# A decoder step on one core: V and K projections in eight slices of two channel tiles instead of four quarters of four

## The reference, cut to what matters

```python
m = silu(c) @ w_ada + b_ada                 # 6 parts of 2048: shift, scale, gate, shift2, scale2, gate2
h = rms_norm(x, g_pre) * (1.0 + scale) + shift
z = h @ w_in                                # 2048 -> 4096
q, k, v, u = jnp.split(z, [1024, 2048, 3072], axis=-1)
# rotary on q and k, differential attention (prompt; samples over cached pages), pooling mixer on u
x = x + gate * rms_norm(concat(a, pooled) @ w_out, g_post)
h = rms_norm(x, g_pre_ffn) * (1.0 + scale2) + shift2
x = x + gate2 * rms_norm(square(relu(h @ w_ff1)) @ w_ff2, g_post_ffn)
```

## Time and profile before

| | us |
|---|---|
| median of three runs | 1501.46 |
| lowest, highest | 1495.84, 1509.36 |
| profiled execution | 1498.26 |
| its span, first to last instruction | 1496.6 |
| V/K stage in it, first product to first fill | 43.7 to 199.7 |

### The profile page before, as it was taken

How to read it: one execution, slowest core, us unless ns; L and a number is a source line. 1 busy time by engine, 2 the same in 40 slices (tenths; PEclk the granted TensorE clock), 3 DMA queues, 4 the chain that set the end, 5 groups by cost and what they waited for, 6 DMA issues and landing times.

```text
span 1496.6 us, 26948 instructions
## 1 busy us (share of the span) xinstructions
PE 1443.1 (96%) x10264; PEld 1313.5 (88%) x10264; DVE 798.9 (53%) x1258; ACT 516.9 (35%) x732; POOL 102.5 (7%) x177
## 2 busy tenths in 40 slices
PE   5999999999899998999999999999999999999996
PEld 1677777778688877999998999999999999999996
DVE  2555558846756568665434444334555344445554
ACT  2222244333356445333232333322333332333331
POOL 1000000067410000000000000000000000000002
PEclk9999999999999999999999999999999999999998
DMA  9999988889677787445445544445544444444431
GB/s 367 341 322 325 322 306 311 284 310 347 245 296 251 257 280 240 155 140 168 140 147 199 189 147 162 141 159 184 195 157 147 151 158 141 141 154 154 141 113 71
DMA packets 87880, 316.40 MB, mean 211 GB/s; under 512 B 12176, under 2 KB 12432, under 8 KB 87168
## 3 DMA queue, kind: packets, MB, share of 16 engines
q1 hardware_dynamic: 79200, 287.87, 55.9%
q0 software_dynamic: 5216, 22.51, 4.0%
q10 hardware_dynamic: 3392, 5.01, 1.0%
HBM read 309.56 MB, written 5.80 MB: 211 GB/s over the span
## 4 chain that ended last, share of the span: by engine, by line
PE 83%; DVE 5%; DMA 5%; POOL 2%; ACT 2%; issue 2%; POOLq 1%; SPq 0%; DVEq 0%; ACTq 0%
PE bank L1519 69%; PE bank L1583 7%; DMA raw<-in_stream 3%; PE bank L1481 3%; PE bank L1496 2%; DMA k_pages<-in_kc 1%; DVE w_lo L774 1%; DMA pools_out<-u_s 1%; POOL win L1382 1%; ACT w_hi L389 0%; ACT pair L631 0%; DVE back L978 0%; POOLq L1363 0%; DVE pair L1184 0%; ACT h_hi L635 0%
## 5 line engine op out<-in xcount | busy, mean ns | idle before, releaser
L774 DVE TENSOR_TENSOR w_lo<-raw,w_hi 128x1024 fp32r<-128x1024 f32 x352 | 419.6, 1225 | 121.7 <-ACT w_hi L389 119.8
L389 ACT ACTIVATE w_hi<-raw 128x1024 fp32r<-128x1024 f32 x352 | 361.6, 1054 | 355.9 <-PE bank L1519 232.8
L1519 PE MATMUL bank<-m_hi,w_hi 128*128 128x320 f32 x1280 | 397.4, 310 | 0.6 <-issue 0.6
L1519 PE MATMUL bank<-m_hi,w_lo 128*128 128x320 f32 x1280 | 395.5, 309 | 0.0
L1519 PE MATMUL bank<-m_lo,w_hi 128*128 128x320 f32 x1280 | 395.5, 309 | 0.0
L1519 PE MATMUL bank<-h_hi,w_hi 128*128 128x320 f32 x1216 | 379.2, 312 | 0.0
L1519 PE MATMUL bank<-h_hi,w_lo 128*128 128x320 f32 x1216 | 375.7, 309 | 0.0
L1519 PE MATMUL bank<-h_lo,w_hi 128*128 128x320 f32 x1216 | 375.6, 309 | 0.0
L1519 PEld LDWEIGHTS bank<-m_hi,w_hi 128*128 128x128 f32 x1280 | 240.3, 188 | 14.6 <-issue 14.6
L1519 PEld LDWEIGHTS bank<-h_hi,w_hi 128*128 128x128 f32 x1216 | 228.2, 188 | 24.1 <-issue 24.1
L1519 PEld LDWEIGHTS bank<-m_lo,w_hi 128*128 128x128 f32 x1280 | 240.3, 188 | 0.0
(11 more groups left out here) (234 smaller groups left out, 1093.8 us busy)
## 6 DMA issues: line engine op xcount, KB each, us to landing
raw<-in_stream SPq DMA_DIRECT2D x544, 512.0 KB, 4.9
k_pages<-in_kc POOLq DMA_DIRECT2D x16, 512.0 KB, 9.2
v_pages<-in_vc POOLq DMA_DIRECT2D x16, 512.0 KB, 7.3
x<-in_x_cm ACTq DMA_DIRECT2D x1, 2560.0 KB, 12.1
x<-in_x_cm POOLq DMA_DIRECT2D x1, 2560.0 KB, 11.3
v_out<-v_cm POOLq DMA_DIRECT2D x1, 1280.0 KB, 9.7
k_out<-back POOLq DMA_DIRECT2D x1, 1280.0 KB, 9.8
y_out<-x SPq DMA_DIRECT2D x2, 640.0 KB, 3.0
```

The lines of the kernel that those rows point to most:

```text
L389: act.activation(w_hi[2 * (j % 2) + h][:, :], raw[slot][:, h * 1024:(h + 1) * 1024], ACT.Copy).then_inc(hi_ready, 1)
L774: dve.tensor_tensor(w_lo[q][:, :], raw[slot][:, h * 1024:(h + 1) * 1024], w_hi[q][:, :], ALU.subtract).then_inc(slot_used[slot], 1)
L1519: last = pe.matmul(bank[j % 2][:, 0:T], w[q][:, k * P:(k + 1) * P], v[:, 8 * h + k, :], start=(h == 0 and k == 0 and n == 0), stop=(h == 1 ...
```

## The change

The contraction of the V/K stage is cut into eight slices of two channel tiles (`SLICES`). A product chunk is now eight output tiles by two channel tiles; each output tile is six matmuls, so there are 128 adds to v_cm and k_cm instead of 64, over the same four banks. Twelve stream chunks still make two slices: products at places `SLICED` = 0, 3, 6, 9, A chunks at 1, 2, 4, 5 for the first and 7, 8, 10, 11 for the second slice. Each slice has one modulation block of its own, with two tiles of scale and two of shift (`MOD_TILES`), so only block 0 (four A chunks) stands ahead of the V/K stage. The u tiles f 8 to 11 get `DENSE` places, so that the number of chunks stays 272. x is loaded in four pieces on SP's queue, ahead of the stream. The prompt tokens are modulated by ACT, scale and shift in one instruction for each tile; POOL still does the sample tokens. PE sums the squares before its first A chunk. The loops over quarters on ACT and DVE are written out.

```diff
-STREAM = 8 + 12 * QUARTERS + 12 * Q_GROUPS + 8 * (U_GROUPS + OUT_GROUPS) + 36 * GROUPS
+SLICES = 2 * QUARTERS
+STREAM = 4 + 12 * QUARTERS + 12 * Q_GROUPS + 12 + 8 + 8 * OUT_GROUPS + 36 * GROUPS
+SLICED = [0, 3, 6, 9]
+SLICED_ADA = [[1, 2, 4, 5], [7, 8, 10, 11]]
+NORMED = [(0, 2), (2, 4), (4, 8), (8, 12), (12, 16)]
 DENSE = [2, 5, 8, 11]
-DENSE_ADA = [[0, 1, 3, 4], [6, 7, 9, 10]]
...
     @block.sync
+        for g in range(4):
+            sp.dma_start(x[:, 4 * g:4 * g + 4, :], x_cm[:, 4 * g:4 * g + 4, :]).then_inc(x_loaded[g], 16)
...
     @block.scalar
-        act.dma_start(x[:, :, :], x_cm).then_inc(x_loaded, 16)
...
+        def slice_h(n):
+            act.wait_ge(gate_done, n + 1)
+            act.wait_ge(normed_s, normed_by(n))
+            act.wait_ge(mod_done, n + 2)
+            for k in range(2):
+                tile = normed[:, 2 * n + k, 0:NP_]
+                act.activation(tile, tile, ACT.Identity, bias=mod[:, n, 2 + k, 0:1], scale=gate[:, 2 * n + k, 0:1]).then_inc(
+                    prompt_mod, 1)
+            act.wait_ge(prompt_mod, 2 * n + 2)
+            act.wait_ge(sample_mod, n + 1)
+            act.activation(h_hi[:, 2 * n:2 * n + 2, :], normed[:, 2 * n:2 * n + 2, :], ACT.Copy).then_inc(h_hi_s, 1)
...
+        for n in range(SLICES):
+            second, following = slice_chunks(n)
+            for h in range(2):
+                hi_half(*second, h)
+            ada_copy(n + 1, quarter_use(n // 2), SLICED_ADA[n % 2][3])
+            hi_half(*following, 0)
+            if n + 1 < SLICES:
+                slice_h(n + 1)
+            hi_half(*following, 1)
...
     @block.vector
+        def sum_tiles(n, jj, h):
+            half = 4 * n + 2 * jj + h
+            for i in range(4):
+                if i < 3:
+                    dve.wait_ge(first_done, 3 * half + i + 1)
                 else:
+                    dve.wait_ge(half_free, half + 5)
+                tile = (v_cm, k_cm)[jj][:, 4 * h + i, :]
+                dve.tensor_tensor(tile, QUARTER_BANKS[i][:, 0:T], tile, ALU.add).then_inc(bank_free[i], 1)
...
+        for n in range(SLICES):
+            second, following = slice_chunks(n)
+            for h in range(2):
+                lo_half(*second, h)
+                sum_tiles(n, 0, h)
+            if n + 1 < SLICES:
+                slice_gate(n + 1)
+            else:
+                mod_add(n + 1)
+            lo_half(*following, 0)
+            sum_tiles(n, 1, 0)
+            if n + 1 < SLICES:
+                low_of_h(n + 1)
+            sum_tiles(n, 1, 1)
+            lo_half(*following, 1)
...
     @block.tensor
-        for a in range(3):
+        sum_parts(0)
+        mean_of_parts(0)
+        for a in range(4):
             ada_chunk(0, 0, a, a)
-        sum_parts(0)
-        ada_chunk(0, 0, 3, 3)
-        mean_of_parts(0)
         pe.wait_ge(tables_loaded, 48)
         ada_turn(0)
-        for a in range(4):
-            ada_chunk(1, 1, a, a)
-        ada_turn(1)
...
+            for i in range(2):
+                nb, places = 2 * g + (i + 1), SLICED_ADA[i]
+                ada_chunk(nb, use, places[0], 0)
+                pe.wait_ge(h_ready, 2 * g + (i + 1))
+                slice_tiles(i, 0, 0, range(4))
+                ada_chunk(nb, use, places[1], 1)
+                ada_chunk(nb, use, places[2], 2)
+                slice_tiles(i, 0, 1, range(2))
+                ada_chunk(nb, use, places[3], 3)
+                slice_tiles(i, 0, 1, range(2, 4))
+                ada_turn(nb)
+                slice_tiles(i, 1, 0, range(4))
+                slice_tiles(i, 1, 1, range(4))
```

More of the change, by code:

```diff
@@ L406, in freed @@
             ins.then_inc(bank_free[j % 2], 1)
-        square_all(x, x_loaded, lambda g: 16)
+        square_all()
         copy_parts(0)
         root(bank[5][:, 0:T], 1, KT / 4)
-        ada_copy(0, 0, 3)
[L413 to L423, removed]
+        def slice_h(n):
[9 more added lines that the diff above has]
+            act.activation(h_hi[:, 2 * n:2 * n + 2, :], normed[:, 2 * n:2 * n + 2, :], ACT.Copy).then_inc(h_hi_s, 1)
@@ L424, in _, with slice_chunks @@
+        ada_copy(0, 0, 3)
+        hi_half(0, quarter_use(0), SLICED[0], 0, 0)
+        slice_h(0)
+        hi_half(0, quarter_use(0), SLICED[0], 0, 1)
         act.dma_start(cos_sin[:, :, :], trig).then_inc(trig_loaded, 16)
-        def quarter(g, following, more):
+        def slice_chunks(n):
+            g, i = n // 2, n % 2
             use = quarter_use(g)
[L429 to L436, removed]
@@ L797, in gate_gain, with low_of_h @@
                 [P, KT, NSEQ]), ALU.mult).then_inc(gate_done, 1)
[L799 to L801 removed]
+        def low_of_h(n):
+            dve.wait_ge(h_hi_s, n + 1)
+            dve.tensor_tensor(h_lo[:, 2 * n:2 * n + 2, :], normed[:, 2 * n:2 * n + 2, :], h_hi[:, 2 * n:2 * n + 2, :],
                               ALU.subtract).then_inc(h_ready, 1)
[L804 to L808, removed]
[L809 to L812 removed]
@@ L875, in _, with slice_gate @@
[L875 to L879, removed]
+        def slice_gate(n):
+            mod_add(n)
+            dve.wait_ge(mod_done, n + 2)
+            dve.scalar_tensor_tensor(gate[:, 2 * n:2 * n + 2, :], mod[:, n, 0:2, :], 1.0,
+                                     gain[:, G_PRE_MIX + 2 * n:G_PRE_MIX + 2 * n + 2].unsqueeze(2).to_broadcast([P, 2, NSEQ]),
+                                     ALU.add, ALU.mult).then_inc(gate_done, 1)
@@ new lines, in times_rstd @@
+        def times_rstd(first, end):
+            dve.tensor_tensor(normed[:, first:end, :], x[:, first:end, :],
+                              rstd[:, :].unsqueeze(1).to_broadcast([P, end - first, T]), ALU.mult).then_inc(normed_s, 1)
+        invert_root(0)
+        for first, end in NORMED[:3]:
+            times_rstd(first, end)
+        slice_gate(0)
+        lo_half(0, quarter_use(0), SLICED[0], 0, 0)
+        low_of_h(0)
+        lo_half(0, quarter_use(0), SLICED[0], 0, 1)
+        for first, end in NORMED[3:]:
+            times_rstd(first, end)
@@ L1328, in _, with modulate_slice @@
         pool.memset(v_cm[:, :, :], 0.0).then_inc(sums_zeroed, 1)
[L1330 to L1337, removed]
-            pool.tensor_tensor(part, part, bcast_seq(shift), ALU.add).then_inc(sample_mod, 1)
-        modulate_part(1, 1, 0, mod[:, 1, :, :])
-        for g in range(1, 4):
-            modulate_part(g + 1, g + 1, g, mod[:, 2 * g + 1, :, :])
-        pool.wait_ge(normed_s, 4)
+        def modulate_slice(n):
+            pool.wait_ge(gate_done, n + 1)
+            pool.wait_ge(normed_s, normed_by(n))
+            pool.wait_ge(mod_done, n + 2)
+            part = seq_view(normed[:, 2 * n:2 * n + 2, NP_:T])
+            mine.then(pool.tensor_tensor(part, part, bcast_seq(gate[:, 2 * n:2 * n + 2, :]), ALU.mult))
+            pool.tensor_tensor(part, part, bcast_seq(mod[:, n, 2:4, :]), ALU.add).then_inc(sample_mod, 1)
+        for n in range(SLICES):
+            modulate_slice(n)
+        pool.wait_ge(normed_s, len(NORMED))
         mine.then(pool.memset(u_p[:, :, 0:HIST], 0.0))
@@ new lines, in slice_tiles @@
+            def slice_tiles(i, jj, h, tiles):
+                j = 2 * i + jj
+                slot, u = use_of(use, SLICED[j])
+                q = 2 * (j % 2) + h
+                pe.wait_ge(slot_used[slot], 2 * u + (3 + h))
+                for b in tiles:
+                    pe.wait_ge(bank_free[b], 8 * g + (2 * j + h + 1))
+                    for k in range(2):
+                        for n, (w, v) in enumerate(((w_hi, h_hi), (w_hi, h_lo), (w_lo, h_hi))):
+                            last = pe.matmul(QUARTER_BANKS[b][:, 0:T], w[q][:, (2 * b + k) * P:(2 * b + k + 1) * P],
+                                             v[:, ds(4 * g + (2 * i + k), 1), :].rearrange("p a t -> p (a t)"),
+                                             start=(k == 0 and n == 0), stop=(k == 1 and n == 2))
+                    last.then_inc(first_done if b < 3 else half_free, 1)
@@ L1607, in fill_half @@
             if h == 0:
[L1608 removed]
+                for nb, place, a in adas if f == 0 else adas[-1:]:
                     chunk_of(nb, use, place, a)
             product_half(c4, use, off, j, h, h_hi, h_lo, h_wait)
[L1611 removed]
+            if h == 0 and f + 1 < 12:
                 nb, place, a = fill_ada(f + 1)[0][0]
```

186 lines of the change are left out of this document (61 added, 125 removed).

## The result

The changed kernel takes 1513.1 us (median of eight runs, 1509.2 to 1518.5), the kernel before 1500.5 beside it (eight runs, 1495.8 to 1509.4). The ratio is 1.0091, 95% interval 1.0074 to 1.0109: 12.6 us more where 2.9 less was forecast, and outside the range. The profiled execution took 1511.2 us, with a span of 1509.5, so 12.9 more than that of before (1496.6).

What follows compares the result with a forecast made beforehand. PE was taken as the bound (busy 96% of the span), with loading bounding the start. Terms -14.2, +4.9, -1.3 and +7.7 sum to -2.9 us, from 1498.26 to 1495.4 us; range 1486 to 1507.

Steps and rivals of the forecast that it cites:

- The start, -14.2: Before the first product: a smaller load ahead of block 0 brings that product to 29.5 from 43.67, -14.2 us.
- if x came second, it would not: At the start: block 0's load hides the mean's chain, with 3 us of slack, only if x loads first.
- A chunks, +4.9: Behind the first product: five more A chunks at 0.98 us lie in PE's way, four in U fills; +4.9 us.
- rival 4: Attention loop: its waits hide 2.9 us of the A chunks, giving 1492.5 us; chance 0.07.
- PE's own work, -1.3: V/K stage: the 768 matmuls stay, and eight switches without an A chunk between save 0.16 each; -1.3 us.
- I take the same after: Behind the first product: the first matmuls run at 1.2 GHz for some 3 us, as before the change.
- The wait at A2, +7.7: V/K slices: A2's slot is freed late by w_lo, so PE waits 1.05 us in seven slices, +0.3 in slice 0.
- rival 2: V/K slices: A2's load takes 6.2 us to land, 2.4 us a slice, giving 1504.8 us; chance 0.18.
- The formula that the prediction takes from the Trainium skill: A2's half-chunk load: 2.0 us plus bytes over 436 GB/s, 3.2 us, which would remove the wait.
- the shortest landing of this trace is 3.7: A2's load: said against a landing of 3.2 us, since no row shows a landing under 3.7 us.
- PE hides them as long as DVE keeps its order: V/K stage: 64 more DVE adds of 0.48 us cost nothing, DVE needing 14 of 19 us a slice.
- Banks freed late: V/K stage: sign of a wrong forecast, PE waiting for DVE's adds within a slice; no size given.

Runs made afterwards that it cites:

- experiment 6: Changed kernel with the four loads of x issued from ACT's queue instead of SP's, ahead of the stream: 1517.5 us, ratio 1.0124 to the kernel before.
- experiment 3: Changed kernel with, in pair 0 only, ACT's exponentials ahead of fill 11's w_hi halves and DVE's w_lo halves behind the second mean copy: 1505.5 us, ratio 1.0034.
- experiment 5: Kernel before the change, with the same turned order in pair 0 as experiment 3: 1501.7 us, ratio 1.0010.
- experiment 4: Changed kernel without modulation block 15 (four A chunks), fills 8 to 11 at their old SUPER places, output not the reference's: 1503.2 us, ratio 1.0018.
- experiment 7: Changed kernel with the turned orders of experiment 1, experiment 2 and experiment 3 together: 1490.1 us, ratio 0.9939 to the kernel before.
- experiment 2: experiment 1 plus, in the last slice, fill 0's w_lo half behind the adds of the K product's first half: 1495.7 us, ratio 0.9985.
- experiment 1: Changed kernel with DVE's second w_lo half of the next product ahead of the last four adds, slices 0 to 6: 1504.2 us, ratio 1.0023.

## Why the prediction was wrong, step by step

- **The start, -14.2.** Right: -14.4, each time within 1 us (22.04 for 23.0; POOL 1.34 + 0.46 for 1.7; 29.24 for 29.5), though two misses, -1.0 and +0.7, nearly cancel. The condition "if x came second, it would not" fits experiment 6, at 4.7 us.
- **A chunks, +4.9.** Not settled. From the last V/K product to the first pooling product, with pair 0 mended (experiment 3), it takes 206.6 us. That is 2.3 more than before (204.3), and 4.7 more than the kernel of experiment 5 (201.9). Both have the old chunks, so the scatter is as large as the question. It is also 3.3 more than in experiment 4 (203.3), which has four A chunks less there. All five paid in full, or half of them hidden as in rival 4: both fit.
- **PE's own work, -1.3.** The V/K stage is 1.5 (experiment 7) or 1.9 (experiment 2) shorter than before, but that it lies so near the forecast is luck: three misses cancel. A slice without a wait takes 18.89 and half a quarter took 19.22, so own work is -0.33 a slice, -2.6 in eight. The slow clock behind the first product, "I take the same after", did not come: the first 24 matmuls took 5.26 us before (43.67 to 48.93) and 3.71 after, another -1.5. And slice 0 waits for its first A2 for 1.7 us (1.29 + 0.22 in experiment 2, 1.47 + 0.19 in 7) and pays a late half chunk, where 0.3 was forecast.
- **The wait at A2, +7.7.** The place, the cause and the landing were right (T + 7.3 for T + 7.2), and experiment 1 shows the cause. The size was not: 1.7 us a slice, so 12 in seven. The mis-sized term is the half chunk, taken as half of 0.98, when a half that comes late costs 1.03. The row that says so was already on the page: the earlier trace rows show both halves of the start at 1.03, x4. The decision point of rival 2, 1.5 us a slice, is passed, but not by rival 2's mechanism (landings of 6.2; here 4.87). The formula that the prediction takes from the Trainium skill (DMA: Bandwidth & Descriptors, Anatomy of one DMA) is stated there for transfers issued from GpSimd, and the stream's are issued from SP; and "the shortest landing of this trace is 3.7" holds for the stream's halves, not for every transfer (two stores of 640 KB landed in 3.0 at the median).
- **"PE hides them as long as DVE keeps its order", at nothing.** This step failed, at the last slice. The sum counted DVE's work (14 of 19 us) and followed its order through one slice in the middle. The last slice has another chunk behind it (fill 0's, freed by A2 itself) and nothing between its w_lo and the adds: +2.3, and 4.35 with a spell of slow clock when the slices before it are faster. "Banks freed late" was named as what would make the forecast wrong, but not priced.
- **The four A chunks moved to the U fills.** They were counted as four times 0.98 of PE work. That they also move fill 11's product to a slot that is freed late, on queues where exponentials stand behind that product, was not looked at. This step failed too, and it is the largest error: +10.5, more than a wait of 3.5 us would suggest, since the slow clock follows it. What stands behind a moved product in each queue was followed for the V/K stage, and left out for the place the chunks went to.

With the measured sizes the sum closes, as it nearly must, since most of them are read off the same two traces: -14.4, V/K 12.0 + 2.3 - 1.5 = +12.8, pair 0 +10.5, A chunks and the rest +4.2 (2.5 and 1.3 of the table, and 0.4 of its pair stage beside the 10.5) make +13.1 against 12.9 measured. The sum was off by 15.8. Pair 0 and the last slice, both outside it, are 12.8 of that, and A2 is 4.3; start, own work and A chunks give back about 1.

What stays open: slices in the kernels of experiments 3 and 4 scatter more (20.4 to 21.9 us) than in the changed kernel, though the V/K stage is the same code. By that the span of a single profiled execution is uncertain by 3 us or so; the timed ratios and the stretches carry the verdicts. How long the clock stays low after a wait (7 to 14 us after much the same one) is open too, and with it the price of pair 0.

## What to carry to other kernels

When chunks change places in a stream with slots in turn, list for each product chunk that moved: which work frees its slot, when, and what ACT and DVE have queued behind its copy. A copy that stands ahead of work the matmul engine waits for is free only while its chunk is early, so put it behind that work, above all at the seams of a schedule (last slice, first pair), which an average period does not show. And price a late piece by the row of such a piece, not as a fraction of the whole.

## What the runs showed of the hardware

- The four matmuls of an A chunk, which write to different row groups of a bank, took 0.97 to 1.10 us together (eight records), and two of them alone (four records) 1.03: half of the set gained nothing.
- A PE wait of 3.5 us in pair 0 was followed by over 13 us at 1.2 GHz (granted clock 0.50 from 333 on, 1.00 at 346), during which the same 96 matmuls took 6.38 instead of 3.71 us. Waits of 3.9 and 3.3 us at the same place (experiments 2 and 6) were followed by about 7 us at 0.50. Waits of 0.3 us in each slice left the clock at 1.00, and so did the one of 2.26 us in the last slice. The Trainium skill (TensorE: Matmul & The Clock Gate, What's actually happening) says that the clock has two levels, half and full, and that it is the half one after idling. The rows agree as far as they go: 0.50 and 1.00, the former behind the long waits, but in experiment 7 also behind one of 1.24 us that left it at 1.00 elsewhere.
- One core's loads ran at 410 to 416 GB/s over 10 us (stream and cache pages together), and a half chunk issued into that took 8.04 us, against 4.87 in the thin queue of a slice.
